# Two transformer blocks on one core: the FFNs' last down projections in one accumulation, the first v loads joined in, copies, sums and row rounds moved

## The chip, the cores and the metric

The kernel runs on one core of a Trainium2 chip. The metric is the device time of the program in microseconds (us); the median of several runs is compared. One further execution was recorded by the hardware profiler; all durations and positions below are from that record.

## The reference, cut to what matters

All data is float32, 512 tokens of width 1024.

Block 1: `mod = silu(c) @ w_ada` gives six vectors of 1024; `h = rms_norm(x) * (1 + sc1) + sh1`; `proj = h @ w_in` (latents for MLA attention, and q, k, v, gate for retention); the two mixers; `x += gt1 * (mixed @ w_out)`; then `h2 = rms_norm(x) * (1 + sc2) + sh2` and a PEER layer: for every token and each of 8 heads the 16 best of 16384 experts are chosen, `a = gelu(u[expert] . h2)`, `x += gt2 * sum(gate * a * v[expert])`. Then an rms norm.

Block 2 (two layers): `h += mixer(rms_norm(h))`, `h += ffn(rms_norm(h))`. Layer 0's mixer is a pooling mixer, layer 1's ("mix1") is differential attention with `qkv = x @ w_qkv` and rope on q and k. The FFN is `g, u = split(x @ w_up)`, a convolution over three neighbouring tokens on g, `(gelu(conv(g)) * u) @ w_down`, with an inner width of 2816, that is 22 tiles of 128 (`FT = 22`). A last rms norm ("final2") ends it.

## The kernel before

**Tiles and precision.** Activations lie transposed: `xT[:, k, :]` is feature tile k (128 features on the partitions, `KT = 8` of them) of 512 tokens. Each float32 factor of a large product is split into a rounded part H and a remainder L; `three` (L376 to L383) issues the three matmuls L·H, H·L and H·H that stand for one product. ScalarE (ACT) writes the H part of each weight chunk (`split_hi`, L344), VectorE (DVE) the L part (`split_lo`, L349).

**Weights** come in chunks of 1 MB through two staging buffers (`STAGES = 2`) into four split slots (`SLOTS = 4`). SyncE (SP) issues the loads in program order: `load(c)` waits for `w_split >= c - 1`, that is until chunk c-2 has been split, and whatever stands behind a waiting instruction of SP's queue waits too. ACT's split of chunk k waits for its landing and for `w_begun`, which TensorE (PE) counts up when it begins a chunk.

**The order of the work is written out by hand, engine by engine**; semaphores join the engines. The stages, in order: ada (DVE sums `w_ada` times silu(c), PE adds over partitions: `mod_cols`, and two chunks' worth of columns directly on PE, L1853) with norm1; first tiles (`C_LAT`, `C_KV`) and eight retention tiles (`C_RQK`), each copied from PSUM by ACT (L632, L637) and turned by rope on DVE (L1081 to L1083), with the rope tables computed by `rope_args` on DVE and `rope_tables` (sine, with a table load) on ACT; MLA and retention; out projection; queries and top-k.

**PEER.** Tokens 128 to 511 are done densely. 64 "u steps" compute gelu(u·h) for 256 experts each, 48 matmuls of 128x384, and store them to HBM (`unit_store`). Over the middle 24 of them (steps 20 to 43, called the W steps here) a gate matrix is built: `hits` writes one-hot blocks for four tokens with three DVE instructions (L1432, L1434, L1436) and `spread_four` on PE (L2086) multiplies them. Then 64 "v steps" (`peer_dve`, `peer_act`, `peer_pe`) multiply stored activations by gates and by v. Tokens 0 to 127 are done row by row: GpSimd (POOL) gathers 128 rows of u and then of v (L1776), DVE does a `row_dot` (L1322) or a `row_sum` (L1329) of 128x1024 with each; their 128 rounds are spread over the u steps and over the v steps. The last v step's products interleave with `gathered` (L2127), which needs all row sums.

**FFN** (twice, `l` = 0 and 1). Unit s0 makes one inner tile: PE two up tiles (48 matmuls of 128x512), DVE the convolution chain (L1618 to L1627), ACT gelu, DVE the product with u and the L part. The down of a unit is 24 matmuls (8 output tiles d, 3 each), each d into its own bank with `start` and `stop`, and DVE adds it to `xT[:, d, :]` (L1594). The last three downs (of units 19, 20, 21) follow each other after the last up tiles, with 24 adds.

**Norms.** ACT squares the 8 tiles, PE sums over partitions, DVE makes the inverse root. In a "column" norm PE uses the squares as weights and a column of ones (L264, a result of 128x1 for each of 4 token tiles and each k), the root is computed on 128x4 and spread by `diagonal` and `spread_root` (L1811). In a "running" norm DVE first adds the eight squares, so that PE sums once. mix1's norm was neither: 8 matmuls with 128x128 ones (L1805) into 128x512, and the root on 128x512 (L956 to L960, L999). final2 was column, not running. Both stood on PE between the last down and what follows.

## Time and profile before

| | |
|---|---|
| median of 3 runs | 2954.36 us (2946.03 to 2956.54) |
| the profiled execution: device time | 2943.87 us |
| the profiled execution: span | 2942.1 us |
| PE busy | 2740.6 us (93%), mean granted clock 0.957 |
| DVE busy | 2237.4 us (76%) |
| ACT busy | 950.0 us (32%) |
| chain that ended last, by engine | PE 73%, DVE 17%, DMA 4%, issue 2%, ACT 2% |
| DMA | 515.54 MB, mean 175 GB/s; 350 GB/s and more in the v steps |

Busy time counts when an engine works on an instruction; a matmul's record overlaps the next one's, so two matmuls that follow each other start about 0.23 us apart (128x512) though each is 0.39 us long. The granted clock is given in parts of full speed: 1.00 is 2.4 GHz, 0.50 is 1.2 GHz. The stages that the change touches begin near 0, 763, 1200, 1740, 2150 and 2870 us of the span.

### The profile page before, as it was taken

The page shows a single profiled execution, that of the slowest core. Times are in us where ns is not written, and L with a number is a line of the kernel's source. Part 1 is how long each engine was busy: PE and PEld are TensorE (multiplying, and loading weights), DVE is VectorE, ACT ScalarE, POOL GpSimd, SP SyncE. Part 2 cuts the span into 40 slices and gives each one's busy share as a digit, 9 for nine tenths or more (in the row PEclk, how much of TensorE's full clock was granted, in tenths as well). Part 3 has the DMA queues.
Part 4 walks back from the last instruction along what each step waited for, and adds up shares of the span by engine and source line. Part 5 has one row for each costly group of instructions (what it writes and reads, how often), then busy time and mean ns, then how long its engine had stood idle before and what let it go on. Part 6 is the DMA issues. An engine that isn't in the chain of part 4 may idle for free.

```text
span 2942.1 us, 38559 instructions
## 1 busy us (share of the span) xinstructions
PE 2740.6 (93%) x13661; PEld 2338.5 (79%) x13661; DVE 2237.4 (76%) x3584; ACT 950.0 (32%) x1238; POOL 385.4 (13%) x275
## 2 busy tenths in 40 slices
PE   6987789997999999999999997999999987999998
PEld 5653457897999999999999994888877832788886
DVE  6467747999899977678888878778786465577786
ACT  3221433342444433333333322222233254322222
POOL 0000000013122244333333330000000000000000
PEclk9986899999999999999999997999999998999998
DMA  5235002256787799999999970223222200132221
GB/s 220 92 111 179 33 29 74 88 210 208 263 297 294 289 356 364 353 340 355 340 348 349 345 281 36 93 86 107 86 79 100 87 14 1 52 106 93 98 102 51
DMA packets 159036, 515.54 MB, mean 175 GB/s; under 512 B 11744, under 2 KB 77664, under 8 KB 127328
## 3 DMA queue, kind: packets, MB, share of 16 engines
q1 hardware_dynamic: 109840, 326.62, 31.3%
q0 software_dynamic: 36864, 134.23, 12.6%
q10 hardware_dynamic: 12240, 53.48, 4.5%
q8 instruction: 55, 0.90, 0.1%
q14 instruction: 37, 0.30, 0.0%
HBM read 461.86 MB, written 52.43 MB: 175 GB/s over the span
## 4 chain that ended last, share of the span: by engine, by line
PE 73%; DVE 17%; DMA 4%; issue 2%; ACT 2%; POOL 0%; SPq 0%; DVEq 0%; ACTq 0%
PE ps L379 21%; PE ps L383 21%; PE ps L382 21%; PE ps L2086 3%; DVE sb_wL L349 2%; DMA sb_stage<-w_ada_l 1%; DMA sb_rows<-u_rows,sb_row_at 1%; PE ps L264 1%; PE ps L2273 1%; DVE sb_stats L1714 1%; DMA sb_stage<-v_l 1%; DVE sb_rows L1322 1%; PE ps L2016 1%; DVE sb_ada_sum L1181 1%; PE ps L1805 1%
## 5 line engine op out<-in xcount | busy, mean ns | idle before, releaser
L379 PE MATMUL ps<-sb_hL,sb_wH 128*128 128x512 f32 (+1 forms) x2240 | 839.3, 375 | 36.3 <-DVE sb_wL L349 18.8
L383 PE MATMUL ps<-sb_hH,sb_wH 128*128 128x512 f32 (+1 forms) x2240 | 821.8, 367 | 0.0
L382 PE MATMUL ps<-sb_hH,sb_wL 128*128 128x512 f32 (+1 forms) x2240 | 821.2, 367 | 0.0
L349 DVE TENSOR_TENSOR sb_wL<-sb_stage,sb_wH 128x2048 fp32r<-128x2048 f32 (+2 forms) x256 | 536.7, 2099 | 200.6 <-ACT sb_wH L344 199.7
L344 ACT ACTIVATE sb_wH<-sb_stage 128x2048 fp32r<-128x2048 f32 (+2 forms) x256 | 445.5, 1757 | 321.3 <-PE ps L379 168.5
L379 PEld LDWEIGHTS ps<-sb_hL,sb_wH 128*128 128x128 f32 x2240 | 424.4, 189 | 95.8 <-issue 24.8
L382 PEld LDWEIGHTS ps<-sb_hH,sb_wL 128*128 128x128 f32 x2240 | 424.3, 189 | 54.3 <-issue 6.0
L383 PEld LDWEIGHTS ps<-sb_hH,sb_wH 128*128 128x128 f32 x2240 | 423.7, 189 | 50.4
L379 PE MATMUL ps<-sb_waL,sb_wH 128*128 128x384 f32 x1024 | 346.5, 338 | 10.0 <-issue 5.5
L382 PE MATMUL ps<-sb_waH,sb_wL 128*128 128x384 f32 x1024 | 345.4, 337 | 0.0
L383 PE MATMUL ps<-sb_waH,sb_wH 128*128 128x384 f32 x1024 | 345.3, 337 | 0.0
L1776 POOL DMA_INDIRECT sb_rows<-u_rows,sb_row_at x128 | 179.8, 1405 | 730.3 <-DVE sb_rows L1322 380.3
L1594 DVE TENSOR_TENSOR sb_xT<-sb_xT,ps 128x512 f32<-128x512 f32 x352 | 229.7, 684 | 28.8 <-PE ps L383 26.8
L1776 POOL DMA_INDIRECT sb_rows<-v_rows,sb_row_at x128 | 185.6, 1450 | 358.6 <-DVE sb_tok L1329 333.2
L379 PEld LDWEIGHTS ps<-sb_waL,sb_wH 128*128 128x128 f32 x1024 | 193.9, 189 | 11.3 <-issue 5.7
L383 PEld LDWEIGHTS ps<-sb_waH,sb_wH 128*128 128x128 f32 x1024 | 193.7, 189 | 0.0
L382 PEld LDWEIGHTS ps<-sb_waH,sb_wL 128*128 128x128 f32 x1024 | 193.6, 189 | 0.0
L864 ACT ACTIVATE sb_gel<-sb_gcv 128x512 f32<-128x512 f32 x44 | 27.8, 632 | 476.0 <-DVE sb_gcv L1625 476.0
L1329 DVE SCALAR_TENSOR_TENSOR sb_tok<-sb_rows,sb_row_act,sb_tok 128x1024 f32<-128x1024 f32 x128 | 164.0, 1282 | 13.8 <-DMA sb_rows<-v_rows,sb_row_at 5.0
L1322 DVE SCALAR_TENSOR_TENSOR sb_rows<-sb_rows,sb_tok 128x1024 f32<-128x1024 f32 x128 | 152.7, 1220 | 18.6 <-DMA sb_rows<-u_rows,sb_row_at 18.2
L379 PE MATMUL ps<-sb_faL,sb_wH 128*128 128x512 f32 x352 | 141.2, 401 | 6.0 <-DVE sb_xT L1594 6.0
L383 PE MATMUL ps<-sb_faH,sb_wH 128*128 128x512 f32 x352 | 140.2, 398 | 0.0
(350 smaller groups left out, 3272.9 us busy)
## 6 DMA issues: line engine op xcount, KB each, us to landing
sb_stage<-u_l SPq DMA_DIRECT2D x64, 1024.0 KB
sb_stage<-v_l SPq DMA_DIRECT2D x64, 1024.0 KB
sb_stage<-up_l SPq DMA_DIRECT2D x44, 1024.0 KB
g_scratch<-sb_ga ACTq DMA_DIRECT2D x64, 384.0 KB
w_scratch<-sb_wst ACTq DMA_DIRECT2D x12, 2048.0 KB, 8.9
sb_wg<-w_scratch SPq DMA_DIRECT2D x32, 768.0 KB
sb_scr<-g_scratch SPq DMA_DIRECT2D x64, 384.0 KB
sb_stage<-down_l SPq DMA_DIRECT2D x44, 512.0 KB
```

Of the source, the lines that this page charges most:

```text
L264: m = pe.matmul(ps[:, bank + t, 0:weights.shape[1]], sq[:, t * P:(t + 1) * P], weights, start=first, stop=last)
L344: act.activation(wH[k % SLOTS][:, 0:n], stage[k % STAGES][:, 0:n], ACT.Copy).then_inc(w_hi, 1)
L349: dve.tensor_tensor(wL[k % SLOTS][:, 0:n], stage[k % STAGES][:, 0:n], wH[k % SLOTS][:, 0:n], ALU.subtract).then_inc(w_split, 1)
L379: m = pe.matmul(dst, lh, rl, start=first, stop=False)
L382: pe.matmul(dst, ll, rh, start=False, stop=False)
L383: return pe.matmul(dst, lh, rh, start=False, stop=last)
L1181: op = dve.scalar_tensor_tensor(total[:, :], w, sc[:, k:k + 1], total[:, :], ALU.mult, ALU.add)
L1322: dve.scalar_tensor_tensor(rows[r % 4][:, :], rows[r % 4][:, :], 1.0, tok[:, :], ALU.mult, ALU.mult, accum_out=column(row_act, r, i, per)) ...
L1329: dve.scalar_tensor_tensor(tok[:, :], rows[r % 4][:, :], column(row_act, r, i, per), tok[:, :], ALU.mult, ALU.add).then_inc(s_g["used"], 1)
L1594: dve.tensor_tensor(xT[:, d, :], xT[:, d, :], ps[:, 4 + d % 4, :], ALU.add).then_inc(s["added"], 1)
L1776: pool.indirect_dma_start(rows[r % 4][:, :], None, A["u_rows" if r < ROUNDS else "v_rows"], bass.IndirectOffsetOnAxis(ap=row_at[:, r % ROU ...
L2086: m = pe.matmul(ps[:, 4 + g0 % 4, q * P:(q + 1) * P], oneJ[g0 % 4][:, q, :], oneI[g0 % 4][:, q, :], start=True, stop=True)
```

## The change

1. **Start.** The second of two column sets of `w_ada` (k = 1) goes from PE (16 of the 32 matmuls of L1853) to DVE's running sum; `mod`'s first addition and `split_lo(0)` stand ahead of the wait for the last `mod_cols`; the first four tiles go to banks 0 to 3 each; their copies stand ahead of `rope_tables` on ACT, and the splits of chunks 2 and 3 are moved up, with the loads that wait for them.
2. **`hits`.** The is-equal and the multiplication of 128x512 become four `tensor_scalar` of 128x128 with two per-partition scalars; the other is-equal stays.
3. **Row rounds.** 12 instead of 8 in the first four W steps, 8 instead of 12 in the last four u steps; the sums go 0, 2, 4, 4 in the first four v steps and 3 and 3 in the last two (2 in each, and 4 and 4, before).
4. **First v steps.** `peer_dve(0)` and `(1)` stand right behind the split of their v chunk, `peer_act` behind the store of its u step; the first four v loads no longer stand behind the wait for all stores: gate load 2+q waits for its own.
5. **FFN ends.** The last three downs accumulate in one group for each d over eight banks, in a mixed order; one add for each d is left (`last_adds`), joined with the norm's work (`folded_low` for mix1, `running_sum` for final2). Unit 21 has buffers of its own (`lastH`, `lastL`).
6. **mix1's norm** becomes running and column: its sums stand behind the third product tile on PE, its spread inside the fourth; the first two tiles are done as a `pair`. Four matmuls and a copy for the v part's root fall away.
7. **final2** becomes running: 4 instead of 32 sums on PE.

```diff
-ROUNDS_A, ROUNDS_W, ROUNDS_C, ROUNDS_V = 20, 8, 12, ROUNDS // 16
+ROUNDS_A, ROUNDS_B, ROUNDS_W, ROUNDS_C, ROUNDS_L, ROUNDS_V = 20, 12, 8, 12, 8, ROUNDS // 16
+FIRST_C = ROUNDS_A + ROUNDS_B + ROUNDS_W * ((W_END - W_FIRST) // 4 - 1)
+FIRST_SUMS = (0, 0, 2, 6, 10)
...
-        COLUMN = ('norm1', 'norm2', 'final2')
-
-        RUNNING = ('norm2', 'ffn1')
+        COLUMN = ('norm1', 'norm2', 'mix1', 'final2')
+
+        RUNNING = ('norm2', 'ffn1', 'mix1', 'final2')
...
                 if j == 1:
-                    sp.wait_ge(s_ada["summed"], KT + 1)
+                    sp.wait_ge(s_ada["summed"], KT + 2)
                 sp.dma_start(ada[3][:, half], A["w_ada_l"][KT - 1][:, half]).then_inc(ld_ada[3 - 2 * j], 16)
...
+            for q in range(4):
+                load(sp, C_V + 3 + q, A["v_l"][q + 3])
+                sp.wait_ge(s_u[f"st{q % 2}"], 16 * (q // 2 + 2))
+                gate_load(2 + q)
+                if q % 2 == 1:
+                    spread_load(3 + q)
             for par in range(2):
                 sp.wait_ge(s_u[f"st{par}"], 16 * (PEER_STEPS // 2))
-            with sp.Fori(0, PEER_STEPS // 4 - 1) as i:
+            with sp.Fori(1, PEER_STEPS // 4 - 1) as i:
...
+                if name == "mix1":
+                    for c in beside:
+                        split_hi_at(act, c)
+                    beside = ()
+                if name == "mix1":
+                    return
...
+            split_hi_at(act, 2)
...
-            rope_tables(0, lambda q: rope_r[:, q, :])
             for t in range(4):
-                if t % 2 == 0:
-                    split_hi_at(act, C_LAT + t // 2 + 2)
                 n = P if t < 3 else MLA_QK
                 act.wait_ge(s_turn["proj"], t + 1)
-                act.activation(lat[0:n, t, :], ps[0:n, t % 2, :], ACT.Copy).then_inc(s_turn["copied"], 1)
+                act.activation(lat[0:n, t, :], ps[0:n, t, :], ACT.Copy).then_inc(s_turn["copied"], 1)
+                if t == 1:
+                    split_hi_at(act, 3)
+            rope_tables(0, lambda q: rope_r[:, q, :])
...
                 for m in range(2):
-                    if s == PEER_STEPS - 1:
-                        peer_act(m)
                     unit_gelu(s, m)
                 unit_store(s)
+                if s >= PEER_STEPS - 2:
+                    peer_act(s - PEER_STEPS + 2)
...
             split_hi_at(act, C_QKV)
-            split_hi_at(act, C_QKV + 1)
             norm("mix1", lambda k: xT[:, k, :], KT, dstH=hH, dstL=hL,
-                 ready=(s_f["added"], KT * (FT - 1)))
+                 ready=(s_f["added"], KT * (FT - 3)), beside=(C_QKV + 1,))
             for t in range(16):
                 if t % 2 == 0:
                     split_hi_at(act, C_QKV + t // 2 + 2)
                 act.wait_ge(s_turn["proj"], 12 + t + 1)
-                act.activation(dqk[:, t, :], ps[:, t % 2, :], ACT.Copy).then_inc(s_turn["copied"], 1)
+                act.activation(dqk[:, t, :], ps[:, t % 2 + (0 if t >= 4 else 4 + t - t % 2), :], ACT.Copy).then_inc(s_turn["copied"], 1)
+                if t == 1:
+                    act.wait_ge(s_norm["rec"], n_at("mix1", "rec") + 1)
+                    act.activation(colr[:, 2, :], colr[:, 1, :], ACT.Sqrt).then_inc(s_norm["root"], 1)
...
-                if k < KT - 1 and k % 2 == 0:
+            for k in range(1, KT):
+                if k < KT - 1 and (k % 2 == 0 or k == 1):
                     dve.wait_ge(ld_ada[k // 2], 32)
                 if k == KT - 1:
                     dve.wait_ge(ld_ada[1], 48)
-                ada_part(KT + k, ada_sum1[:, 0:D], KT + k - 1, k == 2)
+                ada_part(KT + k, ada_sum1[:, 0:D], KT + k, k == 1)
...
-                if k == 5:
-                    dve.wait_ge(s_ada["cols"], 2)
-                    chain(dve.tensor_tensor(mod[:, 0:8], ps[:, 2, 0:8], col("b_ada", 0, 8), ALU.add))
...
+            dve.wait_ge(s_ada["cols"], 2)
+            chain(dve.tensor_tensor(mod[:, 0:8], ps[:, 2, 0:8], col("b_ada", 0, 8), ALU.add))
+            split_lo_at(dve, 0)
             dve.wait_ge(s_ada["cols"], 3)
             dve.tensor_tensor(mod[:, 0:8], ps[:, 0, 0:8], mod[:, 0:8], ALU.add).then_inc(s_ada["mod"], 1)
-            split_lo_at(dve, 0)
             dve.wait_ge(s_ada["mod"], 3)
             scale_rows(*norm1, range(KT), lambda k: gain1[:, k:k + 1], hL, hH, lambda k: mod[:, k:k + 1], done=2)
             split_lo_at(dve, 1)
+            split_lo_at(dve, 2)
 
             dve.wait_ge(ld_const, 64)
...
             rope_args(0, lambda q: rope_r[:, q, :], posi[:, :], col("inv64"))
+            split_lo_at(dve, 3)
             rope_sign(0, lambda q: rope_r[:, q, :], col("sign64"))
-            split_lo_at(dve, 2)
-            split_lo_at(dve, 3)
...
-                dve.tensor_tensor(oneI[par], iota4, picked(0), ALU.is_equal).then_inc(v_chain, 1)
-                chain.n += 1
                 dve.tensor_tensor(oneJ[par], iota4, picked(1), ALU.is_equal)
-                dve.wait_ge(v_chain, chain.n + 16 * i)
-                dve.tensor_tensor(oneI[par], oneI[par], picked(2), ALU.mult).then_inc(s_w["hits"], 1)
+                for t in range(4):
+                    at = bass.ds(4 * g0 + t + 64 * i, 1)
+                    op = dve.tensor_scalar(oneI[par][:, t, :], tab[:, IOTA, :], fromsel[:, 0, at], fromsel[:, 2, at],
+                                           ALU.is_equal, ALU.mult)
...
-                    row_dot(ROUNDS_A + ROUNDS_W // 4 * q + r)
-            n0 = chain.n
+                for r in range(ROUNDS_B // 4):
+                    row_dot(ROUNDS_A + ROUNDS_B // 4 * q + r)
...
             dve.wait_ge(s_w["prod"], TD // 4)
-
-            peer_dve(0)
-            peer_dve(1)
+            for q in range(4):
+                split_lo(dve, C_V - 2 + q)
+                if q >= 2:
+                    peer_dve(q - 2)
+                for r in range(ROUNDS_L * q // 4, ROUNDS_L * (q + 1) // 4):
+                    row_dot(ROUNDS - ROUNDS_L + r)
...
-            with dve.Fori(0, PEER_STEPS // 4 - 1) as i:
+            for q in range(4):
+                peer_dve(2 + q)
+                for r in range(FIRST_SUMS[q], FIRST_SUMS[q + 1]):
+                    row_sum(r)
+            with dve.Fori(0, PEER_STEPS // 4 - 2) as i:
                 for q in range(4):
-                    peer_dve(2 + q, i)
+                    peer_dve(6 + q, i)
                     for r in range(ROUNDS_V // 4):
-                        row_sum(ROUNDS_V // 4 * q + r, i, ROUNDS_V)
+                        row_sum(FIRST_SUMS[4] + ROUNDS_V // 4 * q + r, i, ROUNDS_V)
             for s in range(PEER_STEPS - 2, PEER_STEPS):
...
-                for r in range(ROUNDS_V // 2):
-                    row_sum(ROUNDS - ROUNDS_V + (s - PEER_STEPS + 2) * ROUNDS_V // 2 + r)
+                for r in range(3):
+                    row_sum(ROUNDS - 3 * (PEER_STEPS - s) + r)
...
+            last_adds(0, lambda d: folded_low("mix1", lambda k: xT[:, k, :], d, hL, hH))
             split_lo_at(dve, C_QKV + 1)
-            dve.wait_ge(s_f["added"], KT * FT)
-            norm("mix1", lambda k: xT[:, k, :], KT, dstL=hL, dstH=hH)
-            root = scr[:, 6, :].unsqueeze(1).broadcast_to([P, 2, T])
+            for k in range(1, KT):
+                running_sum("mix1", k)
+            norm_root("mix1", KT)
+            dve.wait_ge(s_norm["spread"], 5)
+            root = ps[:, column_banks("mix1")[1], :].unsqueeze(1).broadcast_to([P, 2, T])
             chain(dve.tensor_tensor(rope_d[:, :, :], rope_d[:, :, :], root, ALU.mult))
...
+            def last_add(l, d):
+
+                at = f_at(l, "o") + KT * (FT - 3) + d + 1
+                dve.wait_ge(s_f["o"], at)
+                dve.tensor_tensor(xT[:, d, :], xT[:, d, :], ps[:, (4 + d) % 8, :], ALU.add).then_inc(s_f["added"], 1)
+
+            def last_adds(l, beside):
+
+                dve.wait_ge(s_f["added"], f_at(l, "added") + KT * (FT - 3))
+                for d in range(KT):
+                    last_add(l, d)
+                    if d >= 1:
+                        beside(d - 1)
+                dve.wait_ge(s_f["added"], f_at(l, "added") + KT * (FT - 2))
+                beside(KT - 1)
 
             norm("ffn0", lambda k: xT[:, k, :], KT, dstL=hL, dstH=hH)
...
-            dve.wait_ge(s_f["added"], f_at(1, "added") + KT * FT)
+            last_adds(1, lambda d: running_sum("final2", d) if d >= 1 else None)
...
+                    if name == "mix1":
+                        for t in range(TT):
+                            m = pe.matmul(ps[:, 0, t:t + 1], square(0)[:, t * P:(t + 1) * P], tab[:, ONES, 0:1],
+                                          start=True, stop=True)
...
-            for k in range(2):
-                for f in range(KT):
-                    m = pe.matmul(ps[:, 2, 8 * k + f:8 * k + f + 1], ada[0][:, k * D + f * P:k * D + (f + 1) * P],
-                                  sc[:, k:k + 1], start=True, stop=True)
+            for f in range(KT):
+                m = pe.matmul(ps[:, 2, f:f + 1], ada[0][:, f * P:(f + 1) * P], sc[:, 0:1], start=True, stop=True)
             m.then_inc(s_ada["cols"], 1)
...
-                if t >= 2:
-                    pe.wait_ge(s_turn["copied"], t - 1)
...
-                    product(pe, C_KV, ps[0:n, t % 2, :], slice((t - 2) * P, (t - 2) * P + n), KT, 224, hH, hL,
+                    product(pe, C_KV, ps[0:n, t, :], slice((t - 2) * P, (t - 2) * P + n), KT, 224, hH, hL,
...
-                        pe.wait_ge(s_turn["copied"], t + 3)
+                        pe.wait_ge(s_turn["copied"], t + 1)
...
+            def last_downs(l, c):
+
+                s = s_f
+                begins = {(1, 2): 1, (2, KT - 1): 1, (0, 0): 1}
+                steps = [(0, d) for d in range(6)] + [(1, 0), (1, 1), (0, 6), (0, 7), (2, 0), (2, 1)]
+                for d in range(2, KT):
+                    steps += [(1, d), (2, d)]
+                for n, d in steps:
+                    k, fh, fl = c + 2 * FT - 3 + n, (faH[1], faH[0], lastH)[n], (faL[1], faL[0], lastL)[n]
+                    if d == 0:
+                        chunk(k)
+                        pe.wait_ge(s["lo"], f_at(l, "lo") + FT - 2 + n)
+                    if n == 0 and d < 4:
+                        pe.wait_ge(s["added"], f_at(l, "added") + KT * (FT - 4) + 5 + d)
+                    if n == 0 and d in (4, 6):
+                        pe.wait_ge(s["act"], f_at(l, "act") + FT - 1 + d // 6)
+                    cols = slice(d * P, (d + 1) * P)
+                    m = three(pe, ps[:, (4 + d) % 8, :], wH[k % SLOTS][:, cols], wL[k % SLOTS][:, cols], fh[:, :],
+                              fl[:, :], n == 0, n == 2, (n, d) in begins)
+                    if n == 2:
+                        m.then_inc(s["o"], 1)
...
-                for s0 in range(FT - 2, FT + 1):
-                    ffn_pe(l, c, s0, has_a=False, down=FT + s0 - 1)
+                last_downs(l, c)
...
-            norm("mix1", KT)
...
-                    tile(C_QKV + t // 2, t % 2, ps[:, t % 2, :], s_turn["proj"], halves_of("mix1") if t == 0 else None)
+                    if t == 0:
+                        pair(C_QKV, (ps[:, 4, :], ps[:, 5, :]), s_turn["proj"], halves_of("mix1"))
+                    elif t >= 2:
+                        tile(C_QKV + t // 2, t % 2, ps[:, t % 2 if t >= 4 else 4 + t, :], s_turn["proj"],
+                             inside=(lambda: spread_root("mix1", scr[:, 6, :], 1, 5)) if t == 3 else None)
+                    if t == 2:
+                        norm("mix1", KT)
...
-                    if t == 2:
-                        pe.wait_ge(s_norm["rec"], n_at("mix1", "rec") + 1)
...
-                if j == 0:
-                    pe.wait_ge(s_turn["roped"], 8 + 1)
-                    for q in range(TT):
-                        m = pe.matmul(ps[:, 6, q:q + 1], scr[0:1, 6, q * P:(q + 1) * P], tab[0:1, ONES, 0:1],
-                                      start=True, stop=True)
-                    m.then_inc(s_dv["root"], 1)
```

## Rows read from the trace of the kernel before

**Rows 1.** Windows: busy us (count) of each engine, PEclk, DMA share, GB/s.

```profile
900.00:1000.00 100.00, 100.00 (x674) 100.00 (x673) 98.86 (x142) 44.02 (x59) 20.98 (x16) 1.00 0.80 294
2000.00:2100.00 100.00, 100.00 (x438) 81.79 (x437) 80.11 (x103) 24.94 (x25) 0.00 (x0) 1.00 0.28 94
```

**Rows 2.** Timeline of the start, PE: start, us, instruction, [idle before].

```profile
29.95 6.96 PE L1853 MATMUL ps<-sb_small,sb_ada 128*128 128x1 f32 x32
...
47.52 0.77 PE L379 MATMUL ps<-sb_hL,sb_wH 128*128 128x512 f32 x1 [3.87 <-DVE sb_hL L1037]
```

**Rows 3.** Timeline of the start, DVE.

```profile
37.02 0.17 DVE L1128 TENSOR_TENSOR sb_mod<-ps,sb_vec 128x8 f32<-128x8 f32 x1 [2.95 <-PE ps L1853]
...
43.78 2.28 DVE L349 TENSOR_TENSOR sb_wL<-sb_stage,sb_wH 128x2048 fp32r<-128x2048 f32 x1
```

**Rows 4.** Waits, 0 to 160 us: us in total, times, longest.

```profile
PE ps L379 <- ACT sb_lat L632: 8.6, 1, 8.6
```

**Rows 5.** Window around the third tile's start.

```profile
61.50:76.00 14.50, 5.94 (x18) 4.79 (x19) 10.27 (x13) 5.83 (x6) 0.00 (x0) 0.65 0.22 82
```

**Rows 6.** DVE's groups in the W steps: busy us, mean ns, idle before.

```profile
L1434 DVE TENSOR_TENSOR sb_scr<-sb_tab,sb_fromsel 128x512 f32<-128x512 f32 x87 | 59.2, 680 | 0.0
L1322 DVE SCALAR_TENSOR_TENSOR sb_rows<-sb_rows,sb_tok 128x1024 f32<-128x1024 f32 x43 | 50.8, 1215 | 0.0
L349 DVE TENSOR_TENSOR sb_wL<-sb_stage,sb_wH 128x2048 fp32r<-128x2048 f32 x22 | 50.3, 2285 | 3.8 <-ACT sb_wH L344 3.8
```

**Rows 7.** DVE's groups over the whole span, forms kept apart.

```profile
L1619 DVE TENSOR_SCALAR sb_gcv<-sb_graw,sb_vec 128x512 f32<-128x512 f32 x44 | 24.1, 547 | 6.8 <-DVE sb_graw L1618 6.3
...
L1253 DVE TENSOR_SCALAR sb_scr<-sb_scr,sb_stats 128x128 f32<-128x128 f32 x8 | 2.3, 287 | 0.3
```

**Rows 8.** Line 1619's instructions and register operations: ns min/median/max.

```profile
L1619 DVEq FUSED_REGOPS  x32: 99/105/123, 1877.8 to 2848.1; - x32
```

**Rows 9.** DVE's timeline in the top-k stage, four short instructions in a row.

```profile
480.08 0.88 DVE L1295 MAX8 sb_topv<-sb_sc_k 128x8 f32<-128x128 f32 x4 [3.51 <-ACT sb_sc_k L735]
```

**Rows 10.** Timeline from u to v: ACT's split of the first v chunk.

```profile
1209.95 1.92 ACT L344 ACTIVATE sb_wH<-sb_stage 128x2048 fp32r<-128x2048 f32 x1 [7.88 <-DMA sb_stage<-v_l]
```

**Rows 11.** SP's queue from u to v.

```profile
1214.22 14.27 SPq L333 DMA_DIRECT2D sb_stage<-v_l  x2
```

**Rows 12.** Waits of PE, 1060 to 1330 us.

```profile
PE ps L379 <- issue: 5.5, 1, 5.5
PE ps L379 <- DVE sb_waL L1481: 2.3, 2, 1.2
```

**Rows 13.** Window at the first v step.

```profile
1225.00:1230.00 5.00, 5.00 (x23) 5.00 (x23) 2.80 (x3) 2.33 (x3) 0.00 (x0) 0.73 0.46 127
```

**Rows 14.** End of the v steps: PE.

```profile
1760.65 0.79 PE L2127 MATMUL ps<-sb_tab,sb_tok 128*128 128x128 f32 x2 [2.74 <-DVE sb_tok L1329]
```

**Rows 15.** End of the v steps: DVE.

```profile
1751.86 1.28 DVE L1329 SCALAR_TENSOR_TENSOR sb_tok<-sb_rows,sb_row_act,sb_tok 128x1024 f32<-128x1024 f32 x1 [1.16 <-DMA sb_rows<-v_rows,sb_row_at]
...
1755.15 5.45 DVE L1329 SCALAR_TENSOR_TENSOR sb_tok<-sb_rows,sb_row_act,sb_tok 128x1024 f32<-128x1024 f32 x4
```

**Rows 16.** End of the first FFN and first qkv tiles: PE.

```profile
2184.78 0.50 PE L379 MATMUL ps<-sb_faL,sb_wH 128*128 128x512 f32 x1 [1.94 <-DVE sb_xT L1594]
...
2203.35 8.59 PE L1805 MATMUL ps<-sb_scr,sb_tab 128*128 128x512 f32 x16
```

**Rows 17.** End of the first FFN: DVE.

```profile
2182.74 0.68 DVE L1618 TENSOR_TENSOR sb_graw<-ps,sb_scr 128x512 f32<-128x512 f32 x1
```

**Rows 18.** End of the fourth qkv tile: PE.

```profile
2235.36 1.02 PE L2232 MATMUL ps<-sb_dqk,sb_tab 128*128 128x512 f32 x2
```

**Rows 19.** End of the second FFN: DVE.

```profile
2910.37 10.12 DVE L1594 TENSOR_TENSOR sb_xT<-sb_xT,ps 128x512 f32<-128x512 f32 x16
2929.94 0.16 DVE L978 TENSOR_SCALAR sb_colr<-ps 128x4 f32<-128x4 f32 x1 [9.46 <-PE ps L264]
```

**Rows 20.** End of the second FFN: PE.

```profile
2923.44 6.38 PE L264 MATMUL ps<-sb_tab,sb_scr 128*128 128x1 f32 x32 [0.17 <-ACT sb_scr L570]
```

87 lines of the change are left out of this document (35 added, 52 removed).

## The prediction, made before the change was run

> **What bounds the kernel now.** I read the windows of 100 us first, for the stages in which PE has no gaps; then, at each place that the diff touches, the waits, and the timeline of each engine. In the W steps PE is busy throughout and DVE for 98.9 us of 100; in the FFN loop PE is busy throughout with 438 matmuls, 0.228 us each, and DVE for 80 [rows 1]. So there only PE's work counts, as long as DVE stays under it. Time is to be had where stages join: PE stands for one of ACT's copies at the first tiles, for DVE's halves at the first v step, for row sums at the last one, and it works on norms that nothing else overlaps after both FFNs [rows 4, 12, 14, 16, 20]. The change touches all of these. I go through them in order of time.
>
> **Start (A).** DVE stands 2.95 us for the 32 column matmuls, which take 6.96 [rows 2, 3]. With 16 of them, 3.5 us, they are done before DVE comes. DVE has one more piece of 128x1024; its first, k = 1, falls into the wait for the next landing, and what is left is that k = 2 becomes a multiply-add, about 0.5 us more (an estimate from 1.2 for such an instruction [rows 6]). Saved: 2.95 + 0.2 of a small addition - 0.5 = 2.6. `split_lo(0)`, 2.28 us [rows 3], stood between the last `mod` and the first L half; now it runs while PE does the last `mod_cols`: 1.9 more. The first product, at 47.52 [rows 2], starts near 43.0: **-4.5**.
> The third tile waits 8.6 us for ACT's copy of the first [rows 4], since ACT stands in `rope_tables` for the whole of `rope_args`. Now it has its own bank, and chunk 1 is split by then, so PE goes on; of the record's 8.6 I count the 8.2 by which the stream stops. Behind the gap the clock is down: 0.65 over 14.5 us, with 24 matmuls in 8.0 instead of 5.5 us [rows 5]: 2.5 more. What is late next is chunk 3's L half, behind `rope_args`; by my sum it is ready near 68 and wanted at 79. The decay loads of ACT's queue keep their place, and the loads of chunks 3 and 4 go out earlier. Everything to the PEER stage hangs on this chain, with no load at a fixed time. A = -4.5 - 8.2 - 2.5 = **-15.2**; between -11 (nothing of the first piece) and -17.
>
> **W steps (B).** PE has 48 matmuls of a unit and 32 of 128x128 a step; 674 in 100 us [rows 1] make 11.9 us a step of 80. DVE's instructions follow each other about 0.08 us before the record of the last ends, so now: 4 x 3 x 0.60 + 2.2 + 2 x 1.15 = 11.7 [rows 6]. The new instruction appears nowhere. Nearest: 128x128 with one per-partition scalar 287 ns; a second scalar adds 60 (I take 547 for two at 128x512 against 486 for one) [rows 7], so 0.35 recorded, **0.27 spaced**. Below it is held by 0.22 for the four MAX8 in 0.88 us [rows 9], above by 0.35 + 0.16 = 0.51, if the register work of a step with an address in a register (0.10 [rows 8]) isn't hidden. In the loop such instructions of 0.60 follow each other without a gap, so I take it as hidden. DVE: 4 x (0.60 + 4 x 0.27) + 2.2 + 2.3 = 11.2 a step, under PE's 11.9: no gain, no loss. In the first four steps a third row makes it 12.4: 0.5 over, four times, part of it in the buffers. The 4 rows more in the gathers find DMA at 0.80 [rows 1]. B = **+1**; between 0 and, at 0.51, 4 x 2.64 + 4.5 = 15.1 a step, +3.2 x 24 = +77.
> The Trainium skill (VectorE: DVE Perf Modes, the section on the TRN2 errata) speaks against the edit: SBUF operands pay a fixed latency once an instruction, so many small tiles pay it many times; it gives (N + 151) cycles for a float32 tensor_tensor. The trace agrees on the size: 0.68 us at 512. By an estimate from that page a two-rate instruction of 128 takes (64 + 151)/0.96 = 0.22 us, four 0.9, against the 1.2 that two large ones cost; by the row four cost 1.1. Both stay below PE.
>
> **From u to v (C).** The first v chunk's H part waits 7.88 us for its load and starts at 1209.95 [rows 10]. DVE then does four row dots and the next split before `peer_dve(0)`; PE stands 5.5 us, then twice 1.2 for L halves [rows 12], and works for 5 us at a low clock (0.73 and below [rows 13]): another 2.5. Together 10.4. Now `peer_dve(0)` follows its split: L part at 1214.1, halves about 1216.5, and PE's last unit ends at 1218.2. This gap goes. The next ones come nearer: v chunks 3 and 4 are issued late, the second load of the SP row only after 14.27 us [rows 11], since it stood behind the wait for all stores. That wait is off it, but chunk 4's load still needs chunk 2 split, and two buffers make each load, H and L a chain of 12 us (7 to 8 + 1.9 + 2.2). From the split of chunk 0 at 1214: chunk 2 split near 1227, chunk 4 near 1238, halves of step 2 near 1240; PE wants them at 1235. Before they came at 1243.5. By this chain alone: -3.3. Four fewer gathers of 0.5 MB ahead of it (2 MB at 0.35 MB a us, 5.7 us of DMA that is full there) bring v chunk 0 and all behind it about 4 us earlier. C = -3.3 - 4 = **-7**; between -3 and -10.4.
>
> **Last v steps (D).** PE stands 2.74 us for the last row sums [rows 14] and restarts at a lower clock (0.66 for 5 us, 1.7 lost). DVE's sums: the first four wait for gathers (1.16 for the last of them), the last four take 5.45 us [rows 15]. With 3 and 3 the sums end about 3.5 us sooner, at 1757 on this scale, and PE is ready at 1758. D = -2.74 - 1.3 = **-4**; between 0 and -5.
>
> **First FFN's end and mix1 (E).** The last up tiles end at 2179.9. The 72 matmuls of the downs take 16.8 at 0.233 each, but end at 2203.35: stands of 1.94 and less for adds [rows 16], as banks are few, and six of them at half clock. Now no add is waited for. The order runs 24 matmuls (5.6 us) to 2185.5 and then wants unit 21's `act`; that chain starts at 2182.74 [rows 17] (rope tables before it on ACT, unchanged) and gives it at 2187.1 without adds between. A new stand of 1.6, too short for the clock by itself. Then 48 x 0.233: end at 2198.4, **-5.0**.
> The 16 matmul halves of mix1's sums, 8.59 us [rows 16], go from here; the pair runs from 2198.4 to 2209.4, with DVE at 1.3 us for an add and a low half ahead of it. In before the second tile ends at 2222.7: 13.3 so far. Back come 0.7 (the third tile waits for the first copy), 0.9 (4 sums) and 1.1 (spread). And there is a new wait: the rope of tile 0 needs the spread inside tile 3, then the table's product (1.2), a split (2.2) and three passes (2.1), so near 2228.3; PE reaches the permutation that waits for it at 2224.7. It stands **3.6 us**, and such gaps were followed by a low clock: 2.4 more. That permutation, at 2235.4 before [rows 18], comes at 2228.3: 7.1; less the clock 4.7. The four small matmuls and the copy for the v root are worth 0.8. E = **-5.5**; between -2 (clock lost twice) and -9 (DVE 3 us quicker than I think).
>
> **Second FFN's end (F).** Here DVE is ready in time; the downs gain the waits, 2.0. Before, 16 adds run in 10.12 us and the sums end at 2929.8: DVE waits 9.46 us for PE [rows 19], which does 32 column matmuls in 6.38 [rows 20] and as many before. Now the adds go with the downs: last down at 2917.6, add 0.7, square 0.7, running sum 0.7, 4 sums 0.9: 2920.9 against 2929.9. F = -9.0, taken as **-8.7** for a colder clock at the spread; between -6 and -9.5.
>
> **Sum.** -15.2 + 1 - 7 - 4 - 5.5 - 8.7 = -39.4. The profiled execution took 2943.87 (span 2942.1, 1.8 around it), so 2904.5 for its like. The median of before is 2954.36, 10.5 above it, and its three runs span 10.5; I take the sum off the median and lean 2 towards the lower runs: **2913**.
>
> **Rivals.** (1) As summed, 0.70. (2) The joins give only their low ends (A -11, C -3, D 0, E -2, F -6, B +3: -19), DMA holding the v start and new waits the others: 2935. For it: DMA is full there, and E's new wait is the longest I know of. Chance 0.15, shared with a median that falls elsewhere in before's spread. (3) The other side: the one-hot instructions decide. DVE passes PE when one spaces over (11.9 - 4.5 - 2.4)/16 = 0.31 us. At 0.44 the loss is 24 x 2.0 = 49, more than all else gives; at 0.51 it is 77 - 1, a time of 2954 + 77 - 40 = 2991. For it: register work is 0.10 a piece and sits four times in 1.1 us. Against: hidden now. Chance 0.07 for more than 0.44; 0.05 for between, with times of 2920 to 2950. (4) A rule as a rival: gathers issued by POOL starve while DVE runs two-rate instructions; here 16 x 0.35 of 11.9 us a step would hold each gather's issue. As rows show four buffers and a gather asked for every 6 us, a delay of 0.35 each changes nothing; if the dots came late by 1 us each, DVE's slack of 0.7 is gone and 48 dots cost some 15: 2928. Chance 0.03. The Trainium skill (SBUF — State Buffer, on the shared port pair and software descriptors) states the rule; no row here shows it.
>
> **Numbers.** 0.5% is about 15 us, what a measurement of this kernel can tell from no change. Faster by more: 0.70 + most of (2) and (4) and half of the middle of (3) = 0.87; same 0.06; slower 0.07. The range that holds eight in ten reaches from 2898, all joins at their best with low runs, to 2938, into (2).
>
> **What would show it.** A: the third tile directly behind the second, PE's first product near 43. B: the spacing of the `tensor_scalar` rows, and 100 us windows with 674 matmuls. C: no PE gap near 1200, one near the third v step. D: no wait at the last v step. E: downs in 17 to 19 us, PE waiting near the fourth qkv tile. F: 9 us between last down and first output less. Wrong it would be if DVE's idle time in W steps vanished, or if gaps kept their length under other names.

## The result, and the profile after

The changed kernel takes 2910.53 us (median of 4, 2905.49 to 2912.55) against 2950.2 us (median of 4, 2944.0 to 2956.54) for the kernel before on the same chip: a ratio of 0.9866 with a 95% interval of 0.9848 to 0.9884. The forecast was 2913, and 39.4 us less than before. That looks closer than it was. The spans of the two profiled executions, 2909.2 and 2942.1, lie only 32.9 apart, and by the stages five terms of the sum held and one, the step from u to v, did not; a base that was some 5 us high made up for most of it, which is luck. One execution of before, at 3155.45 us and a granted clock of 0.825, is left out of every median here.

The page of after, its span and busy times:

```profile
span 2909.2 us, 38552 instructions
...
PE 2717.1 (93%) x13575; PEld 2322.9 (80%) x13575; DVE 2205.4 (76%) x3758; ACT 950.4 (33%) x1238; POOL 392.4 (13%) x275
```

Windows of after in the W steps and in the FFN loop (columns as in [rows 1]):

```profile
900.00:1000.00 100.00, 100.00 (x671) 100.00 (x671) 93.09 (x212) 43.52 (x58) 20.99 (x16) 1.00 0.81 301
2000.00:2100.00 100.00, 100.00 (x438) 81.76 (x437) 79.97 (x103) 24.10 (x24) 0.00 (x0) 1.00 0.28 94
```

PE makes the same pace as in [rows 1], 671 for 674 matmuls in 100 us in the W steps and 438 in the FFN loop, and is never idle in either. DVE has gone from 98.9 to 93.1 of 100 in the W steps, so it does not set the pace there.

The start of after, PE's timeline, then the last two of PE's four waits up to 150 us (the other two, 12.6 and 5.0, are for ACT's squares and stand in before too, 12.9 and 5.0):

```profile
29.70 3.55 PE L1883 MATMUL ps<-sb_small,sb_ada 128*128 128x1 f32 x16
...
42.60 0.77 PE L382 MATMUL ps<-sb_hL,sb_wH 128*128 128x512 f32 x1 [1.98 <-DVE sb_hL L1062]
```

```profile
...
PE ps L382 <- DVE sb_hL L1062: 2.0, 1, 2.0
PE ps L1871 <- DVE sb_ada_sum L1129: 1.9, 1, 1.9
```

The first product starts 4.9 us earlier than in [rows 2]. The wait of 8.6 us in [rows 4] is in the list no more, and no low clock follows it.

DVE's timeline in a W step of after: the new instructions.

```profile
883.36 1.11 DVE L1458 TENSOR_SCALAR sb_scr<-sb_tab,sb_fromsel 128x128 f32<-128x128 f32 x4
884.38 0.68 DVE L1455 TENSOR_TENSOR sb_scr<-sb_tab,sb_fromsel 128x512 f32<-128x512 f32 x1
```

Four one-hots run from 883.36 to the next instruction at 884.38: 1.02 us, 0.255 each.

From u to v, after. PE, then DVE, ACT and SP; the last line is a window behind the stand. A "stand" is a time in which PE waits; with a numeral, v steps and chunks count from 0, so v step 2 is the third and v chunk 0 holds the first one's weights:

```profile
1226.85 0.69 PE L382 MATMUL ps<-sb_waL,sb_wH 128*128 128x384 f32 x1 [5.73 <-DVE sb_waL L1496]
```

```profile
1222.34 2.29 DVE L352 TENSOR_TENSOR sb_wL<-sb_stage,sb_wH 128x2048 fp32r<-128x2048 f32 x1 [3.57 <-ACT sb_wH L347]
1224.55 1.02 DVE L1491 TENSOR_TENSOR sb_scr<-sb_scr,sb_wg 128x384 f32<-128x384 f32 x2
1225.77 1.03 DVE L1496 TENSOR_TENSOR sb_waL<-sb_scr,sb_waH 128x384 fp32r<-128x384 f32 x2 [0.20 <-ACT sb_waH L840]
```

```profile
1220.32 1.91 ACT L347 ACTIVATE sb_wH<-sb_stage 128x2048 fp32r<-128x2048 f32 x1 [5.08 <-DMA sb_stage<-v_l]
```

```profile
1204.44 0.55 SPq L506 DMA_DIRECT2D sb_scr<-g_scratch  x1
1211.54 0.34 SPq L336 DMA_DIRECT2D sb_stage<-v_l  x1
```

```profile
1226.50:1231.50 5.00, 4.65 (x17) 4.65 (x18) 2.27 (x2) 1.92 (x1) 0.00 (x0) 0.58 0.77 288
```

No wait stands at the first v step any more; PE goes from its last unit (which ends at 1204.5) straight through two v steps, and then stands 5.73 us at the third. On DVE the gate halves of that step (L1491, L1496) come directly behind the split of the chunk two steps on (L352), and that split waits for ACT's, which waits 5.08 us for its load. The granted clock is 0.58 over the 5 us behind the stand, so part of them ran at the lower of the two levels.

The last v steps of after, DVE and PE:

```profile
1739.74 4.06 DVE L1352 SCALAR_TENSOR_TENSOR sb_tok<-sb_rows,sb_row_act,sb_tok 128x1024 f32<-128x1024 f32 x3 [0.31 <-DMA sb_rows<-v_rows,sb_row_at]
```

```profile
1744.26 0.38 PE L2154 MATMUL ps<-sb_tab,sb_tok 128*128 128x128 f32 x2
```

The last three row sums end at 1743.8 and PE does not wait for them; [rows 14] had 2.74 us.

The first FFN's end and the qkv tiles of after, PE and DVE:

```profile
2169.28 0.50 PE L382 MATMUL ps<-sb_faL,sb_wH 128*128 128x512 f32 x1 [1.81 <-DVE sb_fa L1649]
...
2203.32 1.02 PE L1842 MATMUL ps<-sb_scr,sb_tab 128*128 128x512 f32 x2
...
2210.12 1.91 PE L2283 MATMUL ps<-sb_dqk,sb_tab 128*128 128x512 f32 x2 [3.69 <-DVE sb_dqk L1108]
```

```profile
2200.34 0.69 DVE L990 TENSOR_TENSOR sb_scr<-sb_tab,sb_colr 128x512 f32<-128x512 f32 x1
2204.37 1.22 DVE L1699 TENSOR_TENSOR sb_rope_d<-sb_rope_d,ps 128x1024 f32<-128x1024 f32 x1 [3.34 <-PE ps L1842]
...
2207.84 0.68 DVE L1106 TENSOR_TENSOR sb_scr<-ps,sb_rope_d 128x512 f32<-128x512 f32 x1
```

The second FFN's end, DVE and PE:

```profile
2884.52 1.32 DVE L1675 TENSOR_TENSOR sb_xT<-sb_xT,ps 128x512 f32<-128x512 f32 x2 [2.08 <-PE ps L386]
...
2894.16 1.53 DVE L1018 TENSOR_TENSOR sb_scr<-sb_scr 128x512 f32<-128x512 f32 x2
2897.11 0.16 DVE L1000 TENSOR_SCALAR sb_colr<-ps 128x4 f32<-128x4 f32 x1 [1.43 <-PE ps L267]
```

```profile
2895.74 1.33 PE L267 MATMUL ps<-sb_tab,sb_scr 128*128 128x1 f32 x8 [2.22 <-DVE sb_scr L1018]
2899.09 2.08 PE L1842 MATMUL ps<-sb_scr,sb_tab 128*128 128x512 f32 x2 [2.02 <-DVE sb_scr L990]
```

DVE's wait for the sums is 1.43 us where [rows 19] had 9.46, and PE's column sums leave 8 records in 1.33 us, where [rows 20] has the last 32 records in 6.38. One float32 column sum leaves two records in the trace: 4 sums are 8 records, and the 32 sums of before are 64, as sums_undone shows below (x64 in 11.29 us). The 32 of [rows 2] are 16 column matmuls in the same way.

### The profile page after: what moved, and what is told of

Its sections match the earlier page's. It is cut to its first block, busy times and chain, and to the rows that moved or that the text cites. A ratio compares the mean times of both kernels' runs of the same rounds, so it can differ in the third digit from the quotient of the medians.

```text
span 2909.2 us, 38552 instructions
## 1 busy us (share of the span) xinstructions
PE 2717.1 (93%) x13575; PEld 2322.9 (80%) x13575; DVE 2205.4 (76%) x3758; ACT 950.4 (33%) x1238; POOL 392.4 (13%) x275
## 4 chain that ended last, share of the span: by engine, by line
PE 74%; DVE 18%; DMA 4%; ACT 2%; issue 2%; POOL 0%; SPq 0%; DVEq 0%; ACTq 0%
PE ps L382 22%; PE ps L385 22%; PE ps L386 22%; PE ps L2113 3%; DVE sb_wL L352 2%; DMA sb_stage<-w_ada_l 2%; PE ps L2318 1%; DVE sb_stats L1741 1%; PE ps L2043 1%; DMA sb_ada<-w_ada_l 1%; DVE sb_rows L1345 1%; DVE sb_ada_sum L1204 1%; DVE sb_scr L1417 1%; DVE sb_topi L1322 1%; DVE sb_topi L1319 1%
## 5 line engine op out<-in xcount | busy, mean ns | idle before, releaser
L352 DVE TENSOR_TENSOR sb_wL<-sb_stage,sb_wH 128x2048 fp32r<-128x2048 f32 (+2 forms) x256 | 536.8, 2099 | 202.8 <-ACT sb_wH L347 202.0
L1616 DVE TENSOR_TENSOR sb_xT<-sb_xT,ps 128x512 f32<-128x512 f32 x304 | 198.3, 684 | 28.8 <-PE ps L386 27.4
L783 ACT ACTIVATE sb_ga<-ps 128x384 f32<-128x384 f32 x128 | 62.2, 491 | 240.4 <-PE ps L386 208.2
L382 PE MATMUL ps<-sb_faL,sb_wH 128*128 128x512 f32 x336 | 133.2, 396 | 3.3 <-DVE sb_fa L1649 1.8
```

Source lines behind the costliest of these rows:

```text
L352: dve.tensor_tensor(wL[k % SLOTS][:, 0:n], stage[k % STAGES][:, 0:n], wH[k % SLOTS][:, 0:n], ALU.subtract).then_inc(w_split, 1)
L382: m = pe.matmul(dst, lh, rl, start=first, stop=False)
L783: act.activation(ga[s0 % 2][:, m, :], ps[:, 2 * (s0 % 2) + m, 0:TD], ACT.Gelu).then_inc(s_u["gelu"], 1)
L1616: dve.tensor_tensor(xT[:, d, :], xT[:, d, :], ps[:, 4 + d % 4, :], ALU.add).then_inc(s["added"], 1)
```

## The experiments

Twelve runs followed, the two kernels once more and ten variants of after, four at a time on one chip; the chips differ between the groups. Times below are medians of 4 executions unless said otherwise. The executions of one kernel spread over 4 to 20 us, so most verdicts rest on stages of the one profiled execution. I measure these between instructions that every version has. Where a variant leaves a stage as in after, its profile also shows how much that stage varies by itself.

**after_again: the changed kernel once more.**

> The changed kernel once more. Between the two profiled executions the stages give -32.8 us (start -13.7 by the W steps, W steps 0, u to v 0, last v steps -4.5, first FFN's end -5.9, second -8.6), while the medians lie 39.7 apart. Theory 1: the stages are right and the kernel before varies by some 10 us from run to run, so over more runs the ratio comes to 0.987 to 0.989 and this profile has the same stage times within 2 us each. Rival: the traces left something out that every run has; then the ratio stays at 0.9866 or below and a second profile of before is about 7 us longer in one definite stage.

Median 2914.71 of 6, ratio 0.9882 (0.9861 to 0.9902). So the first ratio stood at the good end. With all the executions of the four comparisons the medians are 2949.3 for before (31) and 2912.4 for after (10): -36.9. The stages repeat within 0.9 us, but for two. From the spread of final1 to the end of the first FFN's loop it is 371.4 us for 369.8. And the v stage is longer, from 1227.09 to the spread at 1773.00, 545.9 us, where the first profile has 540.4. Its waits are hardly longer, 10.2 us in total for 9.1. PE itself is slower (v loop of after, then of after_again):

```profile
1500.00:1600.00 100.00, 100.00 (x579) 100.00 (x578) 81.02 (x85) 34.29 (x36) 34.97 (x25) 1.00 0.96 347
```

```profile
1500.00:1600.00 100.00, 100.00 (x567) 100.00 (x567) 79.30 (x82) 33.37 (x34) 34.76 (x24) 1.00 0.95 340
```

That is 579 and 567 matmuls in 100 us, with PE never idle and the full clock granted in both, in the same program. I come back to it at the end. The theory that the stages are right and before varies held in direction; the expected stage times within 2 us did not.

**before_again: the kernel before once more, one execution.**

> The kernel before once more, for a second profile. Theory 1: a span between 2942 and 2955 us, what differs lies where PE works in short pieces and the granted clock falls at other moments (rows of 260 to 460 us), 0.5 to 3 us in a place, and not in the W, u, v or FFN loops. Rival: one stage is longer by 5 us or more.

2947.3 us, span 2945.5. Up to the last unit of u the two executions agree within 0.6 us. Then PE's waits from u to v:

```profile
PE ps L379 <- issue: 8.9, 1, 8.9
PE ps L379 <- DVE sb_waL L1481: 1.9, 1, 1.9
```

8.9 us before the first v step, where [rows 12] has 5.5. The first v chunk is not the reason: its H part stands at 1209.81, for 1209.95 in [rows 10]. It is the last row dot ahead of `peer_dve(0)`, which waits 3.08 us for its gather of u rows, where the first execution waited 0.39:

```profile
1221.90 1.23 DVE L1322 SCALAR_TENSOR_TENSOR sb_rows<-sb_rows,sb_tok 128x1024 f32<-128x1024 f32 x1 [3.08 <-DMA sb_rows<-u_rows,sb_row_at]
```

The place was not the one expected (attention) but a join of loops, and the size, 3.5 us, is a little over the 3 us that were allowed.

**halves_first: the gate halves ahead of the split, in v steps 2 to 5.**

```diff
 def peer_dve(s0, i=0, has_split=True, late=False):
-    if has_split and s0 >= 2:
+    if has_split and s0 >= 2 and not late:
         split_lo(dve, C_V + s0 + 2, CHUNK, i, 4)
     ...
+    if late:
+        split_lo(dve, C_V + s0 + 2)
 ...
-    peer_dve(2 + q)
+    peer_dve(2 + q, late=True)
```

The same on ACT, whose first loop iteration is written out for it.

> After, with the gate halves of v steps 2 to 5 formed ahead of the split of the chunk two steps on, on ACT and DVE. Theory 1: what holds the third v step is the order on the queues of ACT and DVE, halves behind a split that waits for its load (DVE's L part at 1222.34, halves done at 1226.8, PE ready at 1221.1). With the order turned the halves are there by 1218, the stand of 5.73 us and the low clock behind it (about 2 us) go, and the whole is 6 to 8 us shorter than after: about 2903. Rival: the two staging buffers hold chunk 4 itself, or the gate halves' own loads are late; then PE stands 3 us or more at the fourth or fifth v step and the whole is within 2 us of after.

2907.95 us, 4.4 under the pooled median of after. PE's timeline has the third v step and the seventh:

```profile
1221.34 0.45 PE L382 MATMUL ps<-sb_waL,sb_wH 128*128 128x384 f32 x1 [1.27 <-DVE sb_waL L1500]
```

```profile
1260.43 0.69 PE L382 MATMUL ps<-sb_waL,sb_wH 128*128 128x384 f32 x1 [5.54 <-DVE sb_waL L1500]
```

The 5.73 us have become 1.27 without any load being earlier. So it was the order on the two queues that held the third step. But a new stand of 5.54 us came at the seventh, where the old order begins again behind four row sums. The tenth v step starts 84.0 us behind u's last unit, where after has 85.0, so only 1.0 us is kept, and the expected 2903 was missed for that reason; the rest of the 4.4 lies within the spread of the executions.

**halves_all: the same in all v steps**, with the first steps' sums spread more evenly (`FIRST_SUMS = (0, 1, 4, 7, 10)`); the two edits were not tried apart.

> After, with the gate halves ahead of the split of the chunk two steps on in every v step (halves_first changed steps 2 to 5 alone and met a stand of 5.5 us at step 6, where the old order begins behind four row sums), and the extra row sums of the first steps spread 1, 3, 3, 3. Theory 1: the order on DVE and ACT is what made PE stand. No stand over 1.5 us at any of the first eight v steps; u to spread 5 to 9 us shorter than in the three executions of after (whose v stage differs by 5 us among themselves): about 2904. Rival: DMA, busy for 0.96 of the time there, sets the pace from the u end on; what is not stood at steps 2 to 6 is stood later, and the whole stays at 2908 or above.

2900.69 us (2894.78 to 2904.56), ratio 0.9823 (0.9796 to 0.9851). PE's waits from 1200 to 1300:

```profile
PE ps L382 <- DVE sb_waL L1494: 1.9, 2, 1.0
```

1.9 us in two. PE's timeline has no stand from 1700 to 1760 either, where after stood 2.47 at the third step from the end. That was the same order once more: in after the split of the last chunk waits for a load issued 16.3 us behind the one before (1711.83 and 1695.52), and the halves stand behind that split (DVE's L part at 1720.39, the last of the halves at 1723.82). From the first u step to the spread of final1 the trace has 1200.8 us, against 1206.6 and 1212.8 in the two of after, although this execution ran its v loop at the slower of the two paces. Its tenth v step starts 77.8 us behind u's last unit, where the two of after have 85.0 and 85.4: 7 us less. Theory 1 holds, and DMA does not set the pace of these first steps. (The medians lie 11.7 us apart, although before had its highest median, 2953.1, on the chip of halves_all.)

**peers_late: the halves of v steps 0 and 1 behind the last row dots again.**

```diff
     split_lo(dve, C_V - 2 + q)
-    if q >= 2:
-        peer_dve(q - 2)
     ...
+peer_dve(0)
+peer_dve(1)
```

`peer_act` goes back with them on ACT.

> After, with the gate halves of v steps 0 and 1 behind the last row dots again, as before; the earlier loads of v chunks 3 and 4 stay. Theory 1: the stand before the first v step comes back (5 us, and 2 of low clock) and the one at the third shrinks by as much, because its halves wait for chunk 4 and not for PE: 0 to +2 us over both. Rival: the stands add, +5 to +8.

2911.31 us, no change. PE's waits from 1200 to 1300:

```profile
PE ps L382 <- DVE sb_waL L1496: 3.5, 3, 1.9
PE ps L382 <- issue: 2.1, 1, 2.1
```

2.1 us stood ahead of the first v step, not the expected 5 (chunk 0's H part comes 2.9 us earlier against u's last unit than in before), and the stand at the third is 1.9. From the end of the last unit to the third step's start it is 22.5 us, in after 22.4, and to the tenth step's 85.2 for 85.0. The stands do not add; whatever is won at the first step is stood at the third.

**loads_late: chunks 3 to 6 behind the wait for all stores again.**

```diff
+for par in range(2):
+    sp.wait_ge(s_u[f"st{par}"], 16 * (PEER_STEPS // 2))
 for q in range(4):
     load(sp, C_V + 3 + q, A["v_l"][q + 3])
-    sp.wait_ge(s_u[f"st{q % 2}"], 16 * (q // 2 + 2))
     gate_load(2 + q)
```

> After, with the loads of v chunks 3 to 6 behind the wait for all stores of the gates again, as before. Theory 1: the third v step waits for chunk 4, and its load goes out 0 to 2 us later than in after: the stand there is 6 to 8 us for 5.7, +1 to +3. Rival: SP's wait was the cost of the transition, +5 or more.

2916.71 us (2910.19 to 2925.59), too wide to tell from after. The trace has the stand at the third step at 7.11 us, and 23.7 us from the last unit's end: +1.3. That is no more than this start varies by with the same joins (22.1 to 24.4 in after, after_again, perm_banks, tables_first, hits_wide and hits_halves), so a cost of the loads' place isn't shown, and the rival's +5 is out.

**tables_first: ACT's rope tables ahead of the four copies again, the banks kept.**

```diff
+rope_tables(0, lambda q: rope_r[:, q, :])
 for t in range(4):
     ...
     act.activation(lat[0:n, t, :], ps[0:n, t, :], ACT.Copy)...
-rope_tables(0, lambda q: rope_r[:, q, :])
```

> After, with ACT's rope tables ahead of the copies of the first four tiles again; the four tiles keep banks of their own. Theory 1: the banks bring the gain. PE goes through the four tiles without a stand and waits only at the first RQK tile, from 66.1 until the first copy near 67.4; +1 to +2 us against after by the ada stage. Rival: ACT's order brings it; then PE stands some 8 us again and the clock falls behind it, +8 to +11.

2911.2 us. No wait for a copy is in the list up to 150 us, and the ada columns come at 250.2 for 249.0 and 249.8 in the two of after: +0.4 to +1.3. The nine variants that change nothing up to there have them between 248.3 and 252.1, so no price of ACT's order is shown. A bank for each tile is enough for this part. Whether the order alone would have done it too was not tried.

**hits_wide: the selected one-hots by two instructions of 128x512 again.**

```diff
-for t in range(4):
-    at = bass.ds(4 * g0 + t + 64 * i, 1)
-    op = dve.tensor_scalar(oneI[par][:, t, :], ...)
+dve.tensor_tensor(oneI[par], iota4, picked(0), ALU.is_equal)...
+...
+dve.tensor_tensor(oneI[par], oneI[par], picked(2), ALU.mult)...
```

> After, with the selected one-hots formed as in before by two instructions of 128x512 in place of four of 128x128. Theory 1: PE bounds the W steps either way: 0 to +1 us from step 24 on; in the first four steps, with three row dots each, DVE needs 12.8 against PE's 11.9, up to +4 there. 0 to +4 over the stage. Rival: the narrower form has its own gain beyond these four steps: more than +5.

2917.16 us. From the first u step's stand to the end of the last unit 646.8 us, against 643.9 and 644.6 in the two of after: +2.2 to +2.9. It is lost early, around the first four W steps with their three row dots: in the window from 760 to 800 PE makes 264 matmuls where after makes 272, from 800 to 900 662 where after makes 672, and from 900 on 675, as many as ever. The rival's +5 did not come. (The median lies 4.8 over that of after; part of that is chance, since this profile reaches the first u step late, at 564.87.)

**hits_halves: each one-hot in two instructions of 128x64.**

```diff
+    for h in (slice(0, 64), slice(64, P)):
-    op = dve.tensor_scalar(oneI[par][:, t, :], tab[:, IOTA, :], ...)
+        op = dve.tensor_scalar(oneI[par][:, t, h], tab[:, IOTA, h], ...)
```

> After, with each 128x128 one-hot formed in two instructions of 128x64, eight in place of four a group. Theory 1: an instruction's fixed part rules, a spacing of 0.20 to 0.22 us for 64 elements where 128 take 0.255; DVE then needs 13.3 to 13.9 us a step, PE 11.9: the W steps become DVE's, +34 to +50 us in all. Rival: cost goes by elements (0.13 us each): no change, 0 to +2.

2969.13 us (median of 7), ratio 1.0065 (1.0042 to 1.0088): slower than before. DVE's timeline and a window:

```profile
882.26 1.86 DVE L1459 TENSOR_SCALAR sb_scr<-sb_tab,sb_fromsel 128x64 f32<-128x64 f32 x8
884.05 0.67 DVE L1455 TENSOR_TENSOR sb_scr<-sb_tab,sb_fromsel 128x512 f32<-128x512 f32 x1
```

```profile
800.00:900.00 100.00, 87.53 (x560) 84.55 (x560) 100.00 (x292) 37.22 (x50) 20.08 (x15) 1.00 0.69 253
```

Eight in 1.79 us, 0.224 each. DVE has no idle time and PE makes 560 matmuls for 672. From the first u step's stand to the end of the last unit it is 695.8 us, +51.9. That is 2.16 us in each of 24 steps, a little over the +50 expected, since an instruction takes 0.224 and not 0.20 to 0.22; DVE's sum, 4 x (0.60 + 8 x 0.224) + 4.5 = 14.1, is 2.2 over PE's 11.9.

**perm_banks: the permutations of the third and fourth qkv tiles in banks of their own.**

```diff
-if t >= 3:
+if t == 4:
+    pe.wait_ge(s_turn["roped"], 8 + 1)
+if t >= 5:
     pe.wait_ge(s_turn["roped"], 8 + t - 2)
-pe.matmul(ps[:, 2 + (t - 1) % 2, :], ...)
+pe.matmul(ps[:, 1 + t if t < 5 else 2 + (t - 1) % 2, :], ...)
...
-rope(dqk[:, t, :], ps[:, 2 + t % 2, :], ...)
+rope(dqk[:, t, :], ps[:, 2 + t if t < 4 else 2 + t % 2, :], ...)
```

> After, with the permutations of the third and fourth qkv tiles in banks of their own, so that they don't wait for the rope of tile 0. Theory 1: PE's stand of 3.69 us near 2206 to 2210 and the low clock behind it (2.4 us by my sum) go, 4 to 6 us less than after: about 2905. Rival: DVE is late for the next permutation as well, PE stands as long one or two tiles later, and the whole is within 1.5 us of after.

2908.77 us. PE's waits from 2175 to 2300:

```profile
PE ps L382 <- DVE sb_wL L352: 0.7, 1, 0.7
PE ps L382 <- DVE sb_dv L1711: 0.4, 1, 0.4
```

The 3.69 us are gone. From the FFN loop's end to the second FFN's norm it is 383.3 us, against 390.4 and 389.8: -6.5 to -7.1, up to 1 more than expected. The other variants without this edit have 387.6 to 391.0. The median lies only 3.6 under the pooled one of after: this profile stood longer at the v steps (7.8 us at the third).

**all_mends: halves_all, perm_banks, and the last v load ahead of a gate load on SP.**

> halves_all with perm_banks, and with the last v load issued ahead of the gate load of step 62 on SP (it lands late by the trace: SP issues it 16 us after the one before, where 8 is the rule, since it stands behind a wait for the halves of step 61). Theory 1: the stand of 2.2 to 2.6 us at the last but one v step and 1.5 of low clock go, the qkv stand as in perm_banks: 6 to 8 us less than halves_all, about 2898. Rival: the last load lands no earlier, since DMA is full; then only perm_banks' 4.5 come: 2900 or more with the stand still there.

2899.7 us (2893.27 to 2903.31), ratio 0.9821 (0.9792 to 0.9851), 1 us under halves_all and inside its spread: the expected 6 to 8 us less did not come in the median. By the stages perm_banks' part is there (383.4 for 389.9 in halves_all). The swapped load is issued 8.3 us behind the one before, as expected, and brings nothing, since halves_all had removed that stand already. It is the lowest median tried, some 13 us under after.

**sums_undone: four row sums in each of the last two v steps again, and final2's 32 column sums on PE.**

```diff
-    for r in range(3):
+    for r in range(4):
-RUNNING = ('norm2', 'ffn1', 'mix1', 'final2')
+RUNNING = ('norm2', 'ffn1', 'mix1')
```

The first v steps have two sums each again, and final2's banks and waits go back with its norm.

> After, with two parts undone that lie far apart. The last two v steps have four row sums each again (first steps 2 each): by my sum PE stands 2.7 us ahead of the gathered products and restarts at a lower clock, +3 to +4.5 there; rival: the sums were early enough, 0 to +1. And final2's 32 column sums stand behind the last downs on PE again in place of one running sum of squares on DVE and 4 column sums: +6 to +7 us between the last down and the spread (32 column matmuls in 6.4 against 1.3, less the adds); rival: hidden behind the adds, 0 to +2. Whole: +10 against after, about 2922.

2926.58 us, 14.2 over the pooled median of after for the expected 10. PE's timeline at the last v step and after the last down:

```profile
1750.60 0.79 PE L2154 MATMUL ps<-sb_tab,sb_tok 128*128 128x128 f32 x2 [4.26 <-DVE sb_tok L1352]
```

```profile
2898.66 11.29 PE L267 MATMUL ps<-sb_tab,sb_scr 128*128 128x1 f32 x64
2912.04 2.08 PE L1842 MATMUL ps<-sb_scr,sb_tab 128*128 128x512 f32 x2 [2.09 <-DVE sb_scr L990]
```

PE stands 4.26 us for the row sums, where after has 0 and after_again 1.5 (halves_first, with the same last sums, has 2.1), and restarts slowly. From the last v load's stand to final1's spread it is 47.7 us, for 42.3 and 40.5 in the two of after: +5.4 to +7.2, more than the expected 3 to 4.5. From the second FFN's norm to the last spread it is 379.3 us against 371.7 in both of after: +7.6, where before has 380.4.

Not undone one by one were the first column set and the early addition of item 1, the downs' order of item 5 and mix1's norm of item 6: what they bring rests on the stages of before and after alone.

## Why the prediction came out as it did

The stages of the two first profiled executions, by the prediction's steps:

| step | predicted | measured | from |
|---|---|---|---|
| A start | -15.2 | -13.8 | first u step with a wait, 574.47 and 560.64 |
| B W steps | +1 | +0.1 | from there to u's last unit: 643.7 and 643.9 |
| C u to v | -7 | +0.2 | last unit to the last v load's stand (less D) |
| D last v steps | -4 | -4.7 | from that stand's end to the spread: 47.1 and 42.3 |
| E first FFN's end | -5.5 | -6.0 | 396.4 and 390.4 from the loop's end to ffn1's norm |
| F second FFN's end | -8.7 | -8.6 | 380.4 and 371.7 from there to the last spread |
| sum | -39.4 | -32.8 | |

**A** was right in each piece: 4.9 for 4.5 at the first product, and 15.5 at 176 us for 15.2. What is missing at 560 us lies within what one program varies by there: the eleven profiles whose code is that of after up to the first u step have it between 558.45 and 564.87. Where it goes was not followed. The prediction left the bank and ACT's order together; tables_first shows that the bank is enough.

**B** was right, and in the number that decided it: spaced 0.255 for the 0.27 forecast from the 287 ns row. Its sum for DVE, 11.2 us a step, is 94 of 100, and the window shows 93.1. The threshold of 0.31 for a one-hot was tested from above by hits_halves: at 0.448 for two halves DVE became the bound, and the prediction's own sum, 16 x (0.448 - 0.31) in each of 24 steps, gives some 53 for the 51.9 lost. The Trainium skill (VectorE: DVE Perf Modes, the section on the TRN2 errata) gives a fixed term that many small tiles pay over and over. The trace agrees that a fixed part rules, 0.224 at 64 elements against 0.255 at 128. The estimate from its (64 + 151)/0.96 was 0.224 for 128 elements, 0.03 under the measured spacing; and against the recorded length, on which its formula fits the 128x512 instruction (0.68), it is 0.12 under the 0.34 measured.

**C** failed, and with it the term "Four fewer gathers ... bring v chunk 0 and all behind it about 4 us earlier". The forecast was the third step's start 7.3 us earlier against u's last unit (3.3 by the chain of loads, 4 by the gathers), and no clock lost behind it. Measured are two things.

- That start came 2.9 us earlier, 22.4 us behind the last unit for 25.3. Chunk 0 did come earlier: its H part stands at 1193.16, 3.1 us earlier against u's last unit than in [rows 10]. But "all behind it" did not follow. The third step waits for chunk 4, whose load goes out when chunk 2 has been split (SP's second line above), lands 8.8 us later, and is split ahead of the gate halves. The two links of this chain, from the split of chunk 0 to that of 2 and on to that of 4, were put at 13 and 11 us and took 14.1 and 13.1. With the 1 us that chunk 0 is short of its 4, that is the missing 4.4, but for 0.2.
- The 2.9 were lost again. The stand of 5.73 us is followed by a low clock of its own (0.58 for 5 us, 2.1 lost), where before two stands of 1.2 at v steps had none, and later steps stood 0.7 and less. At the tenth step after is 85.0 us behind u's last unit and before 85.1, in the first profile of each.

So the stand moved from the first v step to the third with its price. From u's last unit to PE's start behind the last v load it is 520.4 us in after, and 525.0 and 522.0 in perm_banks and tables_first, which have the same joins; after_again has 527.7 at the slower of the two paces described at the end, and before has 520.2 and 524.1. A gain of 7 us isn't there. The cause of the stand is shown by halves_first and halves_all: not the loads (loads_late: 1.3 us, within the spread) nor the place of the first two pairs of halves (peers_late: 0), but the order halves-behind-split. With it turned, 7 us come.

**D** was right, 4.7 for 4; in its own second execution before has 46.2, and after_again 40.5; the variants with the same last sums have 39.6 to 43.1, so the size is known to some 2 us. **E** was right in its parts. The stand for unit 21's halves is 1.81 for 1.6 (the first PE line above). The downs end at 2180.6, 4.6 us earlier on the scale of the loop's end, for 5.0. The new stand at the permutation behind the fourth tile is 3.69 for 3.6, and the row of the spread shows the chain as it was laid out: the root's diagonal at 2200.34, the spread on PE at 2203.32 inside the tile, the tables at 2204.37, the rope of tile 0 to 2210. **F** was right as a sum. (Its terms add up to 2920.6, not to the 2920.9 written.) Its parts moved by 1 us: sums_undone gives 7.6 to the sums, and 1.0 is left for the downs, where I had 2.0.

**The base.** "I take the sum off the median" took 2954.36, the median of three. Of 31 executions it is 2949.3. So 2913 came from a base 5 us too high, less the 2 leaned towards the lower runs, less a sum that was 2.5 too large against the medians (36.9) and 6.6 against the traces. That these nearly cancel is luck. Of the rivals none came true as it was put: of the terms of (2) C alone came out low, and lower than its -3, (3) and (4) not at all. For (4), POOL's gathers take 1.31 us each in the window of after as in [rows 1] (20.99 and 20.98 us for 16), and no row dot waits in the W steps. The Trainium skill (SBUF — State Buffer, on the shared port pair and software descriptors) states that such gathers starve beside two-rate DVE instructions; with these instructions, 0.255 us at a time, no run here shows it.

## What to carry to other kernels

When two stands lie on one chain of loads, the first one's removal is worth only what the second one's start moves: follow the chain to the step that is released last, and ask what each in-order engine has queued ahead of it. Work for the step that is next belongs ahead of work for two steps on, also where both are ready "soon". A stand can have two prices, its length and the low clock behind it (here behind 5.73 us, not behind 1.2), and both go with it when it moves. Before a sum is taken off a median, look at the spread of the runs: here it was a quarter of the effect, and a median of three stood 5 us off.

## What the runs showed of the hardware that was not expected

The v loop has two paces. Of fourteen profiled executions, nine make 578 or 579 matmuls of 384 columns in the window from 1500 to 1600 us, and five (after_again, halves_all, all_mends, sums_undone, hits_halves) 567 or 568; in after_again a step takes 8.48 us for 8.32. PE is never idle in either, and the granted clock is 1.00. after and after_again are the same program. The order of the halves doesn't decide it, since both orders are among the five. The u steps and the FFN loop don't differ between after and after_again (463 and 464 matmuls in 80 us, 438 and 437 in 100). Over 55 steps that is some 9 us, about the spread between the executions of one kernel. What sets it was not tried and stays open.
